# A two-layer encoder trunk on one core: latent projections moved to the start of each layer, on the input not yet divided by its RMS

## The chip, the cores and the metric

The kernel runs on one core of a Trainium2 chip. The metric is the device time of one execution in microseconds. The engines are TensorE (PE, with its weight loads as PEld), VectorE (DVE), ScalarE (ACT), GpSimd (POOL) and the DMA queues, of which SyncE (SP) issues all in the kernel before. Each engine works through its own instructions in order and waits on semaphores for the others.

## The reference, cut to what matters

```python
for l in range(DEPTH):                      # 2 layers, x is 256 x 1024, float32
    u = _rms_norm(x, pre_mix_norm_w[l])
    proj = u @ w_in[l]
    qkv_a, z_a, a_a, b_a, cq, ckv, k_rope, gate_logits = _split_cols(proj, PROJ_SIZES)
    qkv_a = jax.nn.silu(_causal_conv(qkv_a, conv_w[l]))
    # q_a, k_a l2-normalised per head; g_a from softplus(a_a), beta_a = sigmoid(b_a)
    o_a = _gated_delta_rule(q_a, k_a, v_a, g_a, beta_a)      # chunks of 64, 8 heads of 128
    o_a = _rms_norm(o_a, gdn_norm_w[l]) * jax.nn.silu(z_a)
    y_a = o_a @ w_branch_a[l]
    q_b = _rms_norm(cq, q_a_norm_w[l]) @ w_uq[l]             # cq: 384 wide; last 64 of a head rotated
    kv_b = _rms_norm(ckv, kv_a_norm_w[l]) @ w_ukv[l]         # ckv: 256 wide; k_rope: 64, rotated
    y_b = _chunk_causal_attention(q_b, k_b, v_b) @ w_branch_b[l]
    gates = jax.nn.sigmoid(gate_logits)
    h = gates[:, :, 0] * y_a + gates[:, :, 1] * y_b
    x = x + _rms_norm(h @ w_out[l], post_mix_norm_w[l])
    u = _rms_norm(x, pre_ffn_norm_w[l])
    x = x + _rms_norm(jnp.square(jax.nn.relu(u @ w_ff1[l])) @ w_ff2[l], post_ffn_norm_w[l])
```

`_rms_norm(x, w)` is x / sqrt(mean(x²) + 1e-6) times w.

## The kernel before, in words

All activations are held transposed, channels on the 128 partitions and the 256 tokens along the free dimension, so x is eight rows of 128 x 256. A product in float32 precision is made of three fast ones: each operand is split into a high part, rounded to the matmul's format, and a low part, the rest. High times high, high times low and low times high are summed in PSUM (lines 511 to 513). Weights arrive in pieces of 128 x 1024 (512 KB) in a ring of four buffers: ScalarE copies out the high part (`split_hi`, L908), VectorE subtracts it for the low part (`split_lo`, L1180), and SP then loads the next piece into the raw buffer. Of a split piece the buffers come free when TensorE has used it.

The work of a layer is a list of jobs (`JOBS`): v, q and k (4 jobs each, 2 pieces a job), `lat` (3 jobs: the key-value latent, then the query latent with the rotary key in the last half), `kn`, `vt` and `uq` (products of the normalised latents), z, gate, ya, yb, out, ff1 and ff2. A job of two pieces is 48 products of 256 columns into one of three PSUM banks in turn; then ScalarE or VectorE empties the bank. Between the jobs stand steps with small work. `schedule()` writes one order, by hand, and every engine walks this same list and does its part of each entry; `late` holds steps that are put in behind the next job (`job` calls `flush`). Splits are tied to the list as well: ahead of a job, both splitting engines first split up to four pieces past the job's last.

A layer opens with `sq` (ScalarE squares x), `sqsum` (VectorE adds), `norm` (TensorE sums over partitions with a matrix of ones, ScalarE takes the root by Ln and Exp, VectorE forms u and ScalarE and VectorE split it). v, q and k jobs follow, each with `conv` on VectorE and `silu` on ScalarE. The 16 gate inputs (a and b) come from 24 narrow products of their own weights behind v0 (`ab`, `logits`), and `gc` sums the log decays. Behind the k jobs come `lat` with `lnexp` (an explicit load of the table set for Ln and Exp), eight head norms `nrm` (POOL squares, TensorE sums, ScalarE Ln and Exp, VectorE multiplies), the latent norms `latn`, `ktrans`, four `decay` steps and `x1`, which prepares the inverse of the triangular matrices; `lvP` is its first product. The angles of the rotation are computed once, ahead of everything, by VectorE, and ScalarE takes the sines.

Of the kernel before, what the change touches and what calls it, by code (L numbers as in the profile page):

```python
# [23 lines left out]
P = 128  # L24
# [31 lines left out]
def jobs_of_a_layer():  # L56
# [3 lines left out]
    for kind, count, pieces in (("v", 4, 2), ("q", 4, 2), ("k", 4, 2), ("lat", 3, 2), ("kn", 4, 0.5), ("vt", 4, 0.5),  # L60
# [39 lines left out]
def schedule():  # L100

    o = [("start", 0), ("sq", 0), ("sq", 1), ("sqsum", 0), ("sq", 2), ("sq", 3), ("sqsum", 1), ("norm", 0)]
# [63 lines left out]
    def fillers():  # L166
        for i in range(1, 6):
# [21 lines left out]
    for _ in fill:  # L189
        pass  # L190
    o += [("sc", 0), ("sc", 1), ("onrm", 0), ("onrm", 1)]
    job("gate", 2)
    o += [("onrm", 2), ("onrm", 3)]
    for n in range(5):
        job("gate", 3 + n)
        if n:
            o.append(("pv", n - 1))
        o.append(("tr", n))
        if n + 2 < 6:
            o.append(("sc", n + 2))  # L200
# [3 lines left out]
    for i in range(4):  # L204
        job("ya", i)
        if i == 0:
            o += [("pv", 4), ("tr", 5)]
        if i == 1:
            o.append(("pv", 5))
# [25 lines left out]
ORDER = schedule()  # L235


def build(nc, x_in, pos_in, w_in, ab_in, prm_in, cst_in, out):
    with ExitStack() as ctx:
# [23 lines left out]
        prm = keep("prm", [P, NPRM])  # L263
# [4 lines left out]
        ab_all = keep("ab_all", [P, DEPTH, KD * 16])  # L268
        ab_hi = keep("ab_hi", [P, KD * 16], F32R)
        ab_lo = keep("ab_lo", [P, KD * 16], F32R)  # L270
# [4 lines left out]
        bias_cols = keep("bias_cols", [P, 2])  # L275
        eps_col, lnscale_col = bias_cols[:, 0:1], bias_cols[:, 1:2]
# [11 lines left out]
        ul = ph("ul", [P, KD, S], 8, F32R)  # L288
        qT = ph("qT", [P, H, S], 16)
# [13 lines left out]
        rl = ph("rl", [P, S], 83)  # L303
        latT = ph("latT", [P, 5, S], 84)
# [10 lines left out]
        abT = ph("abT", [16, S], 116)  # L315
# [31 lines left out]
        pos_i = ph("pos_i", [P, S], 0, I32)  # L347
        ang = ph("ang", [P, 4, S], 8)
# [26 lines left out]
        s_tab, s_x, s_in, s_out = S_("s_tab"), S_("s_x"), S_("s_in"), S_("s_out")  # L375
        s_trig, s_trig_a = S_("s_trig"), S_("s_trig_a")
# [11 lines left out]
        sq_sum_dve, sq_sum_pool = (signal("sq_sum_dve", 2), signal("sq_sum_pool", 2))  # L388
        x_by_pool, x_by_dve, y_add = (signal("x_by_pool", 4), signal("x_by_dve", 4), signal("y_add", 4))
        prm_ready, squared, sumsq, rnorm = (signal("prm_ready", 1), signal("squared", 8), signal("sumsq", 2), signal("rnorm", 4))  # L390
        pre_scaled, u_hi, u_lo, ab_split_hi = (signal("pre_scaled", 4), signal("u_hi", 4), signal("u_lo", 4), signal("ab_split_hi", 1))
        ab_t, ab_t_copied = (signal("ab_t", 1), signal("ab_t_copied", 1))
# [1346 lines left out]
```

## Time and profile before

| | us |
|---|---|
| median of 3 runs | 1131.35 |
| lowest, highest | 1130.5, 1137.35 |
| the profiled execution, its own time | 1130.21 |
| its span | 1128.1 |
| TensorE busy in the span | 1059.5 |
| VectorE, ScalarE, POOL busy | 745.2, 558.2, 149.6 |
| DMA, mean | 145 GB/s |

The span is the time between the first and the last recorded instruction. Matmuls overlap, so their recorded durations (some 280 ns) are longer than the distance from one to the next; where time is counted, the distance is used.

### The profile page before, as it was taken

What the parts mean: (1) busy time and instruction counts of PE and PEld (TensorE: products, weight loads), DVE (VectorE), ACT (ScalarE), POOL (GpSimd) and SP (SyncE); (2) the same over time, 40 slices, a digit from 0 to 9 for tenths busy, and PEclk for the clock granted to TensorE, in tenths of its full rate; (3) what the DMA queues carried; (4) which work ended last, traced back from release to release, by engine and by line L of the source; (5) the groups of instructions that cost most, each with busy time, mean ns of one, the idle gap of its engine ahead of it and who ended that gap; (6) DMA issues with size and microseconds to landing.
All of it is one profiled execution on the core that took longest, in us unless ns stands there. A gap on an engine that the chain in (4) does not pass through costs nothing.

```text
span 1128.1 us, 24201 instructions
## 1 busy us (share of the span) xinstructions
PE 1059.5 (94%) x10624; PEld 1021.3 (91%) x10624; DVE 745.2 (66%) x967; ACT 558.2 (49%) x766; POOL 149.6 (13%) x108
## 2 busy tenths in 40 slices
PE   3999988999999899999969999989999989999996
PEld 3999887999999799999869998879999989999996
DVE  7697764369767687744377878535696666876453
ACT  5556843635644554433256576445446345444341
POOL 0030310012000222200012114000310013221001
PEclk9999999999999999999969999999999998999998
DMA  5445323323466276666424452333235653666661
GB/s 190 153 158 176 124 95 96 115 74 113 138 207 190 85 214 183 189 187 184 127 94 149 151 168 95 132 96 114 61 127 171 185 168 99 211 187 194 187 184 42
DMA packets 45320, 163.98 MB, mean 145 GB/s; under 512 B 5152, under 2 KB 5536, under 8 KB 45088
## 3 DMA queue, kind: packets, MB, share of 16 engines
q1 hardware_dynamic: 45216, 162.44, 46.0%
q8 instruction: 84, 1.38, 0.5%
q14 instruction: 20, 0.16, 0.0%
HBM read 161.37 MB, written 1.05 MB: 144 GB/s over the span
## 4 chain that ended last, share of the span: by engine, by line
PE 76%; DVE 15%; ACT 5%; issue 3%; DMA 0%; POOLq 0%; POOL 0%; SPq 0%; DVEq 0%; ACTq 0%
PE dense L511 22%; PE dense L512 21%; PE dense L513 21%; DVE wlo L1180 4%; PE sides L607 1%; PE sides L738 1%; PE sides L730 1%; ACT rn L919 1%; DVE E L1402 1%; DVE yT L1463 1%; PE sides L648 1%; DVE E L1396 1%; DVE mx L1394 1%; ACT E L1114 1%; DVE E L1392 1%
## 5 line engine op out<-in xcount | busy, mean ns | idle before, releaser
L1180 DVE TENSOR_TENSOR wlo<-raw,whi 128x1024 fp32r<-128x1024 f32 (+1 forms) x304 | 402.1, 1338 | 187.3 <-ACT whi L908 186.8
L908 ACT ACTIVATE whi<-raw 128x1024 fp32r<-128x1024 f32 (+1 forms) x304 | 315.4, 1048 | 252.6 <-PE dense L513 250.9
L511 PE MATMUL dense<-uh,whi 128*128 128x256 f32 x864 | 254.7, 295 | 11.8 <-DVE ul L1205 7.1
L512 PE MATMUL dense<-ul,whi 128*128 128x256 f32 x864 | 245.9, 285 | 0.0
L513 PE MATMUL dense<-uh,wlo 128*128 128x256 f32 x864 | 245.9, 285 | 0.0
L511 PEld LDWEIGHTS dense<-uh,whi 128*128 128x128 f32 x864 | 166.7, 193 | 17.9 <-issue 13.2
L512 PEld LDWEIGHTS dense<-ul,whi 128*128 128x128 f32 x864 | 166.7, 193 | 2.1 <-issue 1.9
L513 PEld LDWEIGHTS dense<-uh,wlo 128*128 128x128 f32 x864 | 166.6, 193 | 0.0
L511 PE MATMUL dense<-fuh,whi 128*128 128x256 f32 x512 | 146.5, 286 | 10.5 <-DVE ful L1477 10.2
L512 PE MATMUL dense<-ful,whi 128*128 128x256 f32 x512 | 145.1, 283 | 0.0
L513 PE MATMUL dense<-fuh,wlo 128*128 128x256 f32 x512 | 145.1, 283 | 0.0
L513 PE MATMUL dense<-fh,wlo 128*128 128x256 f32 x512 | 143.5, 280 | 0.0
L512 PE MATMUL dense<-fl,whi 128*128 128x256 f32 x512 | 143.5, 280 | 0.0
L511 PE MATMUL dense<-fh,whi 128*128 128x256 f32 x512 | 143.5, 280 | 0.0
L511 PEld LDWEIGHTS dense<-fuh,whi 128*128 128x128 f32 x512 | 98.2, 192 | 12.3 <-issue 10.9
L512 PEld LDWEIGHTS dense<-ful,whi 128*128 128x128 f32 x512 | 98.4, 192 | 0.1
L513 PEld LDWEIGHTS dense<-fuh,wlo 128*128 128x128 f32 x512 | 98.1, 192 | 0.0
L511 PEld LDWEIGHTS dense<-fh,whi 128*128 128x128 f32 x512 | 96.4, 188 | 0.0
L513 PEld LDWEIGHTS dense<-fh,wlo 128*128 128x128 f32 x512 | 96.4, 188 | 0.0
L512 PEld LDWEIGHTS dense<-fl,whi 128*128 128x128 f32 x512 | 96.4, 188 | 0.0
L1610 POOL TENSOR_TENSOR fr<-fr 128x512 f32<-128x512 f32 x32 | 46.4, 1451 | 128.1 <-DVE fr L1449 128.1
L1577 POOL TENSOR_TENSOR sq<-sq,sq 128x512 f32<-128x512 f32 x8 | 10.4, 1297 | 323.4 <-ACT sq L1005 323.4
(272 smaller groups left out, 1861.5 us busy)
## 6 DMA issues: line engine op xcount, KB each, us to landing
raw<-weights SPq DMA_DIRECT2D x304, 512.0 KB, 4.1
xT<-x_t SPq DMA_DIRECT2D x1, 1024.0 KB, 5.3
out_t<-xT SPq DMA_DIRECT2D x4, 256.0 KB, 2.3
cst<-consts SPq DMA_DIRECT2D x1, 512.0 KB, 5.7
prm_all<-params SPq DMA_DIRECT2D x1, 150.0 KB, 5.3
pos_i<-pos SPq DMA_DIRECT2D x1, 128.0 KB, 2.1
ab_all<-w_ab SPq DMA_DIRECT2D x1, 128.0 KB, 6.0
cst<-consts SPq DMA_DIRECT2D x1, 2.0 KB, 1.9
```

The source lines that it names most:

```text
L511: mm(o_, h_[:, ws], ahi[:, k0 + k, :], start=is_first, stop=False, skip_group_check=True)
L512: mm(o_, h_[:, ws], alo[:, k0 + k, :], start=False, stop=False, skip_group_check=True)
L513: x_ = mm(o_, l_[:, ws], ahi[:, k0 + k, :], start=False, stop=is_last, skip_group_check=True)
L607: r = mm(side[0][:, 0:S], ones, q_[:, c, :], start=(c == 0), stop=(c == 5))
L648: r = mm(side[g % 3][:, e * P:(e + 1) * P], one_row, gcT[:, t * P:(t + 1) * P], start=True, stop=True)
L730: r = mm(side[e][rows, 16 * g:16 * (g + 1)], LT[rows, g, e, rows], evens(Xq[rows, e, g, :], SIZES[lv]), start=True, stop=True)
L738: r = mm(side[e][rows, 16 * g:16 * (g + 1)], XTq[rows, e, g, :], PBq[rows, e, g, 0:16], start=True, stop=True)
L908: return A(o_, i_, ACT.Copy)
L919: A(out_, in_, ACT.Ln, scale=scale, bias=eps_col).then_inc(rises, 1)
L1114: A(E[n % 2][:], E[n % 2][:], ACT.Exp, scale=float((DK + ROPE) ** -0.5)).then_inc(sm_exp, 1)
L1180: TT(wlo[s][:, 0:w], raw[s][:, 0:w], f32(whi[s][:, 0:w]), ALU.subtract).then_inc(lo_ready, 1)
L1610: G(fr[i % 4][:], fr[i % 4][:], fr[i % 4][:], ALU.mult).then_inc(f_sq, 1)
```

## The change

The `lat` jobs become the first of each layer. They run on x times its gain, split into `xh` and `xl`, without the division by the RMS r. Since the latent norms would divide it out again, only their epsilon has to be scaled: the argument of the root becomes mean(lat²) + 1e-6 r², with `xm` = 1e-6 r² taken as an Exp. The rotary key and the gate inputs are multiplied by 1/r when the bank is emptied. The 16 gate inputs move into the last lat block (its 48 spare columns are zeros); their own weights, products, copy and DMA go. The norm of x stands behind lat 0. Residual addition and split of the next layer's x are interleaved. The rotary key's step `kr` and POOL's `qd` become steps of their own, further back. The angles are computed by POOL, with the sines behind `silu` 0; x is loaded in four parts on SP, parameters, positions and constants on ScalarE's queue. The last ff2 job also splits two pieces of the next layer. Some attention steps stand one job further back.

```diff
-    for kind, count, pieces in (("v", 4, 2), ("q", 4, 2), ("k", 4, 2), ("lat", 3, 2), ("kn", 4, 0.5), ("vt", 4, 0.5),
+    for kind, count, pieces in (("lat", 3, 2), ("v", 4, 2), ("q", 4, 2), ("k", 4, 2), ("kn", 4, 0.5), ("vt", 4, 0.5),
...
-    o = [("start", 0), ("sq", 0), ("sq", 1), ("sqsum", 0), ("sq", 2), ("sq", 3), ("sqsum", 1), ("norm", 0)]
+    o = [("xsplit", 0), ("xsplit", 1)]
...
+    job("lat", 0)
+    o += [("sq", 0), ("sq", 1), ("sqsum", 0), ("sq", 2), ("sq", 3), ("sqsum", 1), ("norm", 0)]
+    job("lat", 1)
+    o.append(("latn", 0))
+    job("lat", 2)
+    o += [("logits", 0), ("latn", 1)]
     for i in range(4):
         job("v", i)
+        o.append(("conv", i))
         if i == 0:
-            o.append(("ab", 0))
-        o.append(("conv", i))
-        if i == 1:
-            o += [("logits", 0), ("silu", 0)]
-        if i:
+            o += [("gc", 0), ("silu", 0), ("trig", 0)]
+        else:
             late.append(("silu", i))
-        if i == 3:
-            o.append(("gc", 0))
...
         late.append(("silu", 8 + i))
         if i == 0:
             o += [("vtrans", 3), ("dt", 3)]
-    job("lat", 0)
     o += [("lnexp", 0), ("nrm", 0), ("nrm", 1)]
-    job("lat", 1)
-    o += [("nrm", 2), ("latn", 0), ("nrm", 3)]
-    job("lat", 2)
+    job("kn", 0)
+    o += [("nrm", 2), ("nrm", 3)]
+    job("kn", 1)
+    job("kn", 2)
     o += [("nrm", 4), ("nrm", 5)]
-    job("kn", 0)
-    o += [("nrm", 6), ("nrm", 7)]
-    job("kn", 1)
-    o.append(("ktrans", 0))
-    job("kn", 2)
-    o += [("ktrans", 1), ("latn", 1)]
     job("kn", 3)
-    o += [("decay", 0), ("decay", 1)]
     job("vt", 0)
-    o.append(("decay", 2))
+    o += [("nrm", 6), ("nrm", 7), ("qd", 0), ("kr", 0), ("ktrans", 0)]
     job("vt", 1)
+    o += [("ktrans", 1), ("decay", 0), ("decay", 1), ("decay", 2)]
+    job("vt", 2)
     o += [("decay", 3), ("zero", 0), ("x1", 0)]
-    job("vt", 2)
     job("vt", 3)
     job("uq", 0)
+    job("uq", 1)
...
-                for c in (0, 1, 4, 5):
+                for c in (0, 1, 4, 5) if w else (0, 1):
...
             def logits(l, _):
 
-                pe.wait_ge(ab_t_copied, due(l, ab_t_copied, 1))
+                pe.wait_ge(dve_evac, l * NDVE_EVAC + evacs_through(FIRST["lat"] + 2)[1])
...
+            def xsplit(l, part):
+
+                for e in (range(2), range(2, KD))[part]:
+                    if e % 2 == 0:
+                        x_there(l, 0, e // 2)
+                    if l == 0 and e == 0:
+                        act.wait_ge(s_prm, 16)
+                    A(xh[:, e, :], xT[:, e, :], ACT.Identity,
+                      scale=prm_all[:, l, PRE_MIX + e:PRE_MIX + e + 1]).then_inc(x_hi, 1)
...
+            def trig(l, _):
+                if l == 0:
+                    act.wait_ge(s_trig, 24)
+                    A(cosT[:], ang[:, 0, :], ACT.Sin).then_inc(s_trig_a, 1)
+                    A(sinT[:], ang[:, 1, :], ACT.Sin).then_inc(s_trig_a, 1)
...
+            def x_low(l, e):
+                dve.wait_ge(x_hi, due(l, x_hi, e + 1))
+                STT(xl[:, e, :], xT[:, e, :], col(l, PRE_MIX + e), f32(xh[:, e, :]), ALU.mult, ALU.subtract).then_inc(x_lo, 1)
...
+                if n:
+                    dve.wait_ge(sq_sum_dve, due(l, sq_sum_dve, 2))
+                    TT(usq[:, 0:2, :], usq[:, 0:2, :], usq[:, 4:6, :], ALU.add).then_inc(sq_sum_dve, 1)
...
+                dve.wait_ge(lat_mm, due(l, lat_mm, n + 1))
+                dve.wait_ge(x_mean, due(l, x_mean, 1))
+                if n:
+                    dve.wait_ge(lat_norm, due(l, lat_norm, 1))
+                STT(rl[:], side[4][:, 0:S], 1.0 / (QL if n else KVL), xm[:], ALU.mult, ALU.add).then_inc(lat_arg, 1)
...
                 times_norm(0)
+                add(0)
                 times_norm(1)
-                add(0)
+                low(0)
                 times_norm(2)
-                low(0)
-                times_norm(3)
                 add(2)
                 low(1)
+                times_norm(3)
                 low(2)
                 low(3)
```

## Rows read from the trace of the kernel before

**Rows 1.** The page: span, busy time of an engine, and one group of instructions

```profile
span 1128.1 us, 24201 instructions
PE 1059.5 (94%) x10624; PEld 1021.3 (91%) x10624; DVE 745.2 (66%) x967; ACT 558.2 (49%) x766; POOL 149.6 (13%) x108
...
L908 ACT ACTIVATE whi<-raw 128x1024 fp32r<-128x1024 f32 (+1 forms) x304 | 315.4, 1048 | 252.6 <-PE dense L513 250.9
```

**Rows 2.** TensorE's waits over the whole span: total us, times, longest

```profile
PE sides L607 <- DVE usq L1192: 21.2, 2, 13.6
...
PE dense L511 <- DVE wlo L1180: 4.4, 4, 1.2
```

**Rows 3.** The chain that ended last, 0 to 120 us: start, us, what

```profile
13.56 3.76 PE sides L607 x8
...
20.84 0.55 PE dense L511
21.39 0.21 PE dense L512
```

**Rows 4.** The same chain, 540 to 720 us, where layer 1 opens

```profile
561.93 0.48 ACT rn L919
...
576.83 0.55 PE dense L511
```

**Rows 5.** Busy time by stretch: PE, PEld, DVE, ACT, POOL, clock, DMA share, GB/s

```profile
80.00:100.00 20.00, 20.00 (x170) 19.71 (x170) 15.31 (x26) 12.22 (x21) 0.00 (x0) 1.00 0.45 144
104.10:156.80 52.70, 48.97 (x336) 42.58 (x335) 38.94 (x65) 38.20 (x62) 15.18 (x12) 1.00 0.35 111
```

**Rows 6.** ScalarE in order of time: start, us, line, operation

```profile
11.54 2.19 ACT L928 ACTIVATE usq<-xT 128x512 f32<-128x512 f32 x4
...
110.42 0.62 ACT L1010 ACTIVATE kT<-kT 128x512 f32<-128x512 f32 x1
111.06 1.28 ACT L1018 ACT_TABLE_LOAD   x1
112.35 0.23 ACT L1021 ACTIVATE sm<-sm 128x32 f32<-128x32 f32 x1
...
112.61 0.67 ACT L919 ACTIVATE rn<-sides,bias_cols 128x512 f32<-128x512 f32 x1
...
115.27 1.99 ACT L908 ACTIVATE whi<-raw 128x1024 fp32r<-128x1024 f32 x2
```

**Rows 7.** VectorE in order of time, in four stretches

```profile
10.73 0.24 DVE L1186 COPY prm<-prm_all 128x150 f32<-128x150 f32 x1
...
18.42 1.67 DVE L1209 SCALAR_TENSOR_TENSOR utmp<-xT,prm,rn 128x256 f32<-128x256 f32 x4 [1.35 <-ACT rn L921]
...
24.19 0.28 DVE L1215 TENSOR_TENSOR ab_lo<-ab_all,ab_hi 128x128 fp32r<-128x128 f32 x1
...
31.70 0.41 DVE L1219 COPY abT<-sides 16x256 f32<-16x256 f32 x1 [3.20 <-PE sides L619]
...
56.41 3.84 DVE L1180 TENSOR_TENSOR wlo<-raw,whi 128x1024 fp32r<-128x1024 f32 x2
...
567.58 1.29 DVE L1186 COPY prm<-prm_all 128x150 f32<-128x150 f32 x1
```

**Rows 8.** Groups of ScalarE's instructions: busy us, mean ns, idle before

```profile
L1010 ACT ACT_TABLE_LOAD x2 | 2.6, 1283 | 0.0
```

**Rows 9.** The chain that ended last, 120 to 300 us

```profile
145.55 0.22 PE sides L708 x2
...
156.81 1.25 PE sides L730 x84
```

**Rows 10.** DMA issues of the page: KB each, median us to landing

```profile
raw<-weights SPq DMA_DIRECT2D x304, 512.0 KB, 4.1
...
out_t<-xT SPq DMA_DIRECT2D x4, 256.0 KB, 2.3
```

More of the change, by code:

```diff
@@ L166, in fillers @@
     def fillers():
-        for i in range(1, 6):
+        for i in range(2, 6):
             job("uq", i)
@@ L190, in schedule @@
         pass
+    job("gate", 2)
     o += [("sc", 0), ("sc", 1), ("onrm", 0), ("onrm", 1)]
-    job("gate", 2)
+    job("gate", 3)
     o += [("onrm", 2), ("onrm", 3)]
-    for n in range(5):
-        job("gate", 3 + n)
+    for n in range(4):
+        job("gate", 4 + n)
         if n:
             o.append(("pv", n - 1))
-        o.append(("tr", n))
-        if n + 2 < 6:
-            o.append(("sc", n + 2))
+        o += [("tr", n), ("sc", n + 2)]
         if n < 2:
@@ L235, with build @@
 ORDER = schedule()
-def build(nc, x_in, pos_in, w_in, ab_in, prm_in, cst_in, out):
+assert [n for what, n in ORDER if what == "job"] == list(range(NJOB))
+def build(nc, x_in, pos_in, w_in, prm_in, cst_in, out):
     with ExitStack() as ctx:
@@ L891, in ysum @@
                 r.then_inc(y_mm, 1)
-            do = dict(norm=norm, ab=ab, logits=logits, dt=dt, job=job, gc=gc, vtrans=vtrans, nrm=nrm, latn=latn, ktrans=ktrans, decay=decay,
+            do = dict(norm=norm, logits=logits, dt=dt, job=job, gc=gc, vtrans=vtrans, nrm=nrm, latn=latn, kr=kr_, ktrans=ktrans, decay=decay,
                       lvP=lvP, lvV=lvV, pairP=pairP, pairV=pairV, lastP=lastP, lastV=lastV, half=half, t_v0=t_v0, t_st=t_st, t_ks=t_ks, t_v1=t_v1, t_o=t_o, onrm=onrm,
                       sc=sc, tr=tr, pv=pv, ysum=ysum, qrope=qrope)
-            pe.wait_ge(s_in, 3 * 16)
             for l in range(DEPTH):
@@ L1147, in fsplit @@
                 copy(fh[:, 2 * i:2 * i + 2, :], fr[i % 4][:]).then_inc(f_hi, 1)
-            do = dict(sq=sq_, squares=squares, norm=norm, fsplit_x=fsplit_x, logits=logits, job=job, silu=silu, vtrans=vtrans, lnexp=lnexp, nrm=nrm, latn=latn,
+            do = dict(xsplit=xsplit, trig=trig, sq=sq_, squares=squares, norm=norm, fsplit_x=fsplit_x, logits=logits, job=job, silu=silu, vtrans=vtrans, lnexp=lnexp, nrm=nrm, latn=latn,
                       decay=decay, x1=x1, pairP=pairP, pairV=pairV, lastP=lastP, lastV=lastV, t_st=t_st, t_o=t_o, onrm=onrm, osplit=osplit, sc=sc, tr=tr, pv=pv, sig=sig,
                       hsplit=hsplit, post=post, fsplit=fsplit)
-            act.wait_ge(s_trig, 12)
-            A(cosT[:], ang[:, 0, :], ACT.Sin).then_inc(s_trig_a, 1)
-            act.wait_ge(s_trig, 20)
-            A(sinT[:], ang[:, 1, :], ACT.Sin).then_inc(s_trig_a, 1)
-            act.wait_ge(s_x, 16)
-            nc.scalar.preload_act_table_set("natural_log_exp_and_others")
+            nc.scalar.preload_act_table_set("natural_log_exp_and_others")
+            act.dma_start(prm_all[:], prm_in).then_inc(s_prm, 16)
+            act.dma_start(pos_i[:], pos_in).then_inc(s_tab, 16)
+            act.dma_start(cst[:, C_FREQ:NCST], cst_in[:, C_FREQ:NCST]).then_inc(s_tab, 16)
+            act.wait_ge(s_x[1], 16)
+            act.dma_start(cst[:, 0:C_FREQ], cst_in[:, 0:C_FREQ]).then_inc(s_in, 16)
+            act.wait_ge(s_bias, 3)
             for l in range(DEPTH):
-                for (what, n), pieces in zip(ORDER, splits_at):
+                for (what, n), pieces in steps_with_splits(l):
                     for p_ in pieces:
-                        split_hi(l, p_)
+                        split_hi(p_)
                     if what in do:
@@ L1494, in fsplit @@
                    f32(fh[:, 2 * i:2 * i + 2, :]), ALU.subtract).then_inc(f_lo, 1)
-            do = dict(start=start, sqsum=sqsum, norm=norm, ab=ab, logits=logits, gc=gc, dt=dt, conv=conv, nrm=nrm, latn=latn, qrope=qrope, ktrans=ktrans,
+            do = dict(xsplit=xsplit, sqsum=sqsum, norm=norm, logits=logits, gc=gc, dt=dt, conv=conv, nrm=nrm, latn=latn, kr=kr_, qrope=qrope, ktrans=ktrans,
                       decay=decay, x1=x1, lvP=lvP, lvV=lvV, t_v0=t_v0, t_v1=t_v1, t_ks=t_ks, onrm=onrm, osplit=osplit, sc=sc, pv=pv, job=job,
@@ L1529, in _ @@
-            dve.wait_ge(s_trig_a, 2)
-            step(TS(sinT[:], sinT[:], cst[:, C_FREQ + 1:C_FREQ + 2], None, ALU.mult))
-            dve.wait_ge(s_x, 16)
-            dve.wait_ge(s_in, 3 * 16)
+            V.memset(eps_col, EPS).then_inc(s_bias, 1)
+            V.memset(lnscale_col, math.log(DK ** -0.5)).then_inc(s_bias, 1)
+            V.memset(lneps_col, math.log(EPS)).then_inc(s_bias, 1)
+            dve.wait_ge(s_prm, 16)
             for l in range(DEPTH):
-                for (what, n), pieces in zip(ORDER, splits_at):
+                for (what, n), pieces in steps_with_splits(l):
```

331 lines of the change are left out of this document (171 added, 160 removed).

## The prediction, on record before the changed kernel ran

> **What bounds the kernel now.** I read the page first: TensorE is busy 94% of the span and ScalarE 49% [rows 1], so the end moves with TensorE's work and its idle time, and with nothing else. The list of waits then says where TensorE idles for another engine: 21.2 us in two waits at the sum of squares that opens a layer, 4.4 us in four for split weights [rows 2]. The chain of waits dates the openings. In layer 0 the norm's products run 13.56 to 17.32 and the first dense product starts at 20.84 [rows 3]; in layer 1 the last sum of layer 0 ends at 561.93, where ScalarE takes over, and the first dense product starts at 576.83 [rows 4]. Products there come 0.21 us apart (1.2 GHz, after TensorE had been idle); in steady state 170 in 20 us, 0.118 us apart (2.4 GHz) [rows 3, 5], so a dense job of 48 costs 5.65 us. Last I looked at the stretch out of which the latent jobs are taken, from the end of the k jobs to the first product of the triangular inverse, 104.1 to 156.8. TensorE is busy 49.0 of its 52.7 us, ScalarE 38.2 [rows 5]: the latent jobs are what fills TensorE while ScalarE works through eight norms.
>
> **The openings.** Before, v0 runs 20.84 to 28.6 and the 24 gate-input products end at about 31.4 (the copy behind them starts at 31.70 [rows 7]). After, x comes in 256 KB parts, first in the queue; a store of that size takes 2.3 us and a weight piece 4.1 [rows 10]. The piece, issued fifth at about 2.6, lands near 7; its split (1.05 on ScalarE [rows 1], some 1.2 on VectorE) lets TensorE start near 9.4 (13.5 if it lands as late as 11). lat0 then takes 7.8 us, as v0 did, to 17.2. But the norm is behind lat0 in every queue: ScalarE waits for lat0, squares the bank (0.6), then x four times (2.19 [rows 6]), VectorE adds three times (1.4 of it after the last square): 21.4. Two of four norm products are left, 1.9 us: 23.3.
>
> From there a chain decides, not TensorE. VectorE normalises x (1.35 for the root, 5.8 for eight products and four low halves, 18.42 to 24.19 [rows 7]), ScalarE splits pieces 5 and 6 only behind it (2.1), VectorE follows with 2.5 and lat1's evacuation 0.8; first latent norm 3.3 over both engines; pieces 7 and 8, 2.8; lat2's evacuation 0.8; logits and second sum 1.9: about 19.7 us, while TensorE has 14.1 of work. v0 would start at 43.0. Before, the same work (norm, three jobs, latent sums 2.2) stands at 31.4 + 11.3 + 2.2 = 44.9.
>
> Into this falls the angle chain, 24 dependent steps on POOL. A POOL instruction holds VectorE up: a copy of 150 columns that takes 0.24 takes 1.29 beside POOL's add, and two splits take 3.84 beside the DT chain [rows 7] instead of twice 1.2. No row has POOL's scalar step. Four of its 512-column operations cost VectorE some 3 us, so 24 of half that width cost at most 9 and, where VectorE has slack, nothing; I take 2. Layer 0 gains 1.9 - 2 = 0 (bounds -7 and +6).
>
> Layer 1: rn at 562.9, first add at 564.2, xh and xl of the first row at 565.2, TensorE starts at 565.3 instead of 576.8 (pieces 0 and 1 are split during the last ff2 job). lat0, mostly at 1.2 GHz and paced by the adds, ends at 573.2. The same late squares put the norm's products at 578.6 and the chain puts v0 at 600.2; before, 587.6 + 11.3 + 2.2 = 601.1. Gain 1 (0 to +5). **So 11.5 us of earlier start per layer come back as two new waits**: some 5 us at the norm, 3.4 at the logits.
>
> The trade shows in VectorE's queue too: the add for xh waits behind lat0's evacuation, and the logits step now waits for lat2's evacuation, with v0 queued behind it. In the v jobs the logits chain no longer delays splits (2.2 us a layer, half of the 4.4 [rows 2]); layer 0 gets the two sines there instead, with a table load before and one after, 3.4 us of ScalarE. I take -2.0 for both layers.
>
> **The middle.** This is the largest term. Taken out of the stretch: three jobs, 16.95, and 10 latent products, 2.2; drawn in: uq1, 18 products, 2.1. Net 17.0 us of TensorE per layer that stand elsewhere; the stretch must shrink by 17.0 to come out even.
>
> silu(11) is appended behind the last k job and issued at the next job. That was lat0, ahead of lnexp(0): Silu at 110.42, the table load at 111.06 [rows 6]. Now it is kn0, and lnexp(0), nrm 0 and nrm 1 stand before it. So ScalarE loads the table for Ln and Exp, does two norms, loads Silu's (at line 1010 a load stands that nobody wrote [rows 8]), and meets Ln again in nrm 2 with Silu's set active. What set an unwritten load for Ln brings no row shows. Low bound: the shared one, two loads more. High bound: one that lacks Exp; then every Ln and Exp of nrm 2 to 7 loads, 12 + 1 = 13. I take the high bound: the source asks for Sigmoid by function, but before every stage that alternates Ln and Exp it asks for the set by name (lines 1018, 1135, 1157), which would be needless if asking for Ln brought both. At 1.283 us each [rows 8], 16.7 us per layer on the engine that paces the norms.
>
> ScalarE's queue from the end of k3: evacuation and silu 10, 2.0; written load and two small Exps 1.6; nrm 0 and 1, 2.65 (112.61 to 115.27 [rows 6]); splits 33 to 35, 2.45; five evacuations 2.4; silu 11 and two qd exponentials 1.5; nrm 2 to 7, 6 x 1.33 = 8.0; 13 loads 16.7: 37.3. TensorE's and VectorE's parts are shorter and each nrm waits for the last Ln. Then in series: last kT product 0.7, ktrans 0.7, decay 0 to 3 of 16 products at 0.11 [rows 9] 4 x 1.78, vt2 1.4, decay 3 on VectorE 1.65, x1 4.9 (the last decay ends near 151.9, the inverse starts at 156.81 [rows 9]): 16.5. That is 53.8; TensorE has then been idle often, and what of it runs at 1.2 GHz adds 0 to 3: 55.3. The stretch grows by 2.6 where it should shrink by 17.0: **loss 19.6 per layer, 39.2** (low bound, two loads: the same walk gives 39.7 for the stretch, a loss of 4.0 per layer).
>
> **Small ones.** The residual step before ff1 reaches its first low half one 0.6 us multiplication earlier: -1.2 for two layers. The last POOL add (1.64) starts one such instruction later: +0.6. kr's work is about equal, the gate inputs' dropped DMA and the prm copy lie beside other work; the attention steps moved behind gate and ya jobs keep 5.65 us of product each as cover: 0; without it a step waits for its softmax, some 3 us.
>
> **Sum**, against the profiled execution's 1130.2: 0 - 1.0 - 2.0 + 39.2 - 1.2 + 0.6 = +35.6: 1165.8. The median of the runs is 1131.35, 1.1 above it: **1167**.
>
> **The skill beside it.** The Trainium skill (ScalarE: Activation LUTs, What ACT_TABLE_LOAD costs) adds a drain of 1.38 us to each switch. Here 111.06 + 1.283 = 112.34 and the next activation starts at 112.35 [rows 6], so the trace disagrees. The same page's rule to group calls by table set speaks against this order. The Trainium skill (GPSIMD Engine Reference, Key points) has GpSimd share its memory interfaces with VectorE; the 1.29 beside 0.24 agrees.
>
> **Rivals.**
> Shared set: the load before nrm 2's Ln brings both. Then 8 stands for 39.2: 1130.2 - 1.0 - 2.0 + 8 - 1.2 + 0.6 = 1134.6, with the median 1136. For it: every load in the trace stays good for a whole stage. Against: the sets named by hand. 0.08.
> Faster: the opening gains survive. Place: between TensorE's early start and v0. If the chain of 19.7 shrinks to TensorE's 14.1 and the wait at the norm stays under 2, each layer keeps 5.6 + 3 more; with shared loads that is 1136 - 17 = 1119. It decides from a chain near 14 us; VectorE's own part of it, 5.8 + 2.5 + 0.8 + 1.7 + 2.5 + 0.8 = 14.1, speaks against. 0.04.
> Slow clock: the idle middle keeps TensorE at 1.2 GHz, so that its 9.2 us of products in series take double (7.7 more than I allowed, per layer), and POOL costs the opening its 7: 1167 + 15 + 7 = 1189. 0.05.
> Drain: each of 26 new loads costs 1.38 more, 1203. 0.01.
> Forecast 0.82. The change does what it says in all of them.
>
> **Range.** Own range: the middle 34 (no slow clock, and a load or two per layer hidden in a wait) to 47, the openings 10 better to 7 worse, the rest 2 either way: 1150 to 1184. It leaves out the rivals and little more. A run of this kernel can tell 1% (11 us) from nothing; slower by over 1%: forecast, slow clock, drain and a part of shared set, 0.89; within: 0.07; faster 0.04.
>
> **What would show it.** Table loads at the norm's Ln and Exp lines, 12 per layer; from the end of k3 to the first inverse product 53 to 58 us with TensorE busy about 31; first dense product near 9.4 and 565, a wait of about 5 behind lat0 and 3 before the logits. It is wrong if loads number two a layer there, or if the stretch ends near 40.

## The result, and the profile after

The changed kernel takes 1188.63 us (median of 4 runs, 1185.69 to 1192.16), the kernel before 1133.05 beside it; the ratio is 1.0488 [1.0442, 1.0534]. The direction was right, the size was not: 1167 was predicted, in a range of 1150 to 1184, so the loss is 55.6 us between these medians and 58.8 between the profiled executions (1130.21 to 1188.98), where the sum had 35.6.

The first rows of the page after, against [rows 1]: TensorE is busy 12 us longer, and idle 46.8 us more (115.4 against 68.6).

```profile
span 1186.8 us, 24158 instructions
PE 1071.4 (90%) x10568; PEld 1027.8 (87%) x10568; DVE 754.3 (64%) x967; ACT 598.2 (50%) x807; POOL 167.4 (14%) x133
```

The list of TensorE's waits after (what waited, for whom: us in total, times, longest) answers [rows 2]. The two waits of 21.2 us are gone. The first row is four waits: 10.7 at the kernel's start, 3.3 in the first latent job of layer 1, and 5.0 ahead of ya0 in either layer. In place of the old two stand 12 waits for Ln in the norms of q and k, one per layer ahead of the key transposes, and in the opening one for the sum of squares and one for the rotary key.

```profile
PE dense L515 <- DVE wlo L1206: 24.0, 4, 10.7
PE sides L669 <- ACT rn L919: 20.6, 12, 3.4
PE sides L693 <- DVE kT L1303: 12.8, 2, 6.9
PE sides L624 <- DVE krx L1468: 9.7, 2, 5.0
PE dense L515 <- DVE ful L1514: 9.6, 2, 4.8
PE sides L617 <- DVE usq L1228: 8.7, 2, 4.4
```

ScalarE's table loads after, by line (count, total us, mean ns), answer [rows 8]: twelve per layer at the norms' Ln (L919) and Exp (L921), and a second per layer at silu (L1029).

```profile
L919 ACT ACT_TABLE_LOAD x12 | 15.4, 1283 | 0.2
L921 ACT ACT_TABLE_LOAD x12 | 15.4, 1283 | 0.2
L1029 ACT ACT_TABLE_LOAD x4 | 5.1, 1283 | 0.1
L1043 ACT ACT_TABLE_LOAD x4 | 5.1, 1283 | 0.1
```

ScalarE's timeline in the middle of layer 0 (start, duration) shows how it comes about, where [rows 6] had one load for the whole stage. Silu's set is fetched for the last k pair; from then on every Ln fetches one set and every Exp another.

```profile
130.49 0.72 ACT L921 ACTIVATE rn<-rn,bias_cols 128x512 f32<-128x512 f32 x1
...
132.66 1.28 ACT L1029 ACT_TABLE_LOAD   x1
133.95 0.63 ACT L1029 ACTIVATE kT<-kT 128x512 f32<-128x512 f32 x1
134.60 1.28 ACT L919 ACT_TABLE_LOAD   x1
135.89 0.69 ACT L919 ACTIVATE rn<-sides,bias_cols 128x512 f32<-128x512 f32 x1
136.60 1.28 ACT L921 ACT_TABLE_LOAD   x1
137.89 0.72 ACT L921 ACTIVATE rn<-rn,bias_cols 128x512 f32<-128x512 f32 x1
```

The same stretch as a window, from the end of k3 to the first product of the inverse, in both layers (length; busy us of TensorE, its weight loads, VectorE, ScalarE, POOL; granted clock; DMA share and rate), answers [rows 5]. It lasts 57.1 us (55.3 predicted, against 52.6 before), ScalarE works 46 of them, TensorE's granted clock is 0.79 and 0.82.

```profile
125.00:182.10 57.10, 39.73 (x199) 30.19 (x197) 28.01 (x51) 45.94 (x62) 13.40 (x12) 0.79 0.18 56
705.50:762.50 57.00, 38.64 (x198) 29.43 (x197) 28.00 (x51) 45.96 (x62) 13.40 (x12) 0.82 0.17 55
```

TensorE's waits in the two openings, as its timeline after has them (start, duration, and in brackets the idle time before and who ended it): at the norm, at the logits, and in layer 1 inside lat0, for the second weight piece. v0 starts at 47.51 and 629.13.

```profile
23.17 1.19 PE L617 MATMUL sides<-usq,cst 128*128 128x256 f32 x2 [4.38 <-DVE usq L1228]
44.19 1.03 PE L624 MATMUL sides<-cst,krx 16*128 16x16 f32 x4 [4.97 <-DVE krx L1468]
...
596.48 0.58 PE L515 MATMUL dense<-xh,whi 128*128 128x256 f32 x1 [3.30 <-DVE wlo L1206]
606.26 1.19 PE L617 MATMUL sides<-usq,cst 128*128 128x256 f32 x2 [4.30 <-DVE usq L1228]
```

Last, a place where the prediction had put nothing: ahead of ya0. After gate 7 ScalarE does the sixth softmax's Exp, loads Sigmoid's table, does four sigmoids and loads the other table back; only then come the two splits that ya0 needs. VectorE's low half and TensorE's wait follow.

```profile
323.69 0.63 ACT L1139 ACTIVATE E<-E 128x512 f32<-128x512 f32 x1 [4.28 <-DVE E L1432]
324.34 1.28 ACT L1154 ACT_TABLE_LOAD   x1
325.63 3.90 ACT L1159 ACTIVATE gates<-gates 128x1024 f32<-128x1024 f32 x4
329.55 1.28 ACT L1160 ACT_TABLE_LOAD   x1
330.84 2.00 ACT L908 ACTIVATE whi<-raw 128x1024 fp32r<-128x1024 f32 x2
...
331.93 2.36 DVE L1206 TENSOR_TENSOR wlo<-raw,whi 128x1024 fp32r<-128x1024 f32 x2 [5.97 <-ACT whi L908]
...
333.21 0.58 PE L515 MATMUL dense<-oh,whi 128*128 128x256 f32 x1 [4.98 <-DVE wlo L1206]
```

### The profile page after: what moved, and what is told of

It is laid out like the page before. It is cut to its first block, busy times and chain, and to the rows that moved or that the text cites. A ratio compares the mean times of both kernels' runs of the same rounds, so it can differ in the third digit from the quotient of the medians.

```text
span 1186.8 us, 24158 instructions
## 1 busy us (share of the span) xinstructions
PE 1071.4 (90%) x10568; PEld 1027.8 (87%) x10568; DVE 754.3 (64%) x967; ACT 598.2 (50%) x807; POOL 167.4 (14%) x133
## 3 DMA queue, kind: packets, MB, share of 16 engines
q8 instruction: 83, 1.36, 0.5%
## 4 chain that ended last, share of the span: by engine, by line
PE 73%; DVE 13%; ACT 9%; issue 4%; DMA 0%; POOL 0%; SPq 0%; POOLq 0%; ACTq 0%; DVEq 0%
PE dense L515 21%; PE dense L517 20%; PE dense L516 20%; DVE wlo L1206 4%; ACT L919 1%; ACT whi L908 1%; ACT rn L919 1%; PE sides L739 1%; ACT rn L921 1%; PE sides L731 1%; PE sides L709 1%; PE sides L710 1%; PE sides L646 1%; DVE E L1432 1%; DVE mx L1430 1%
## 5 line engine op out<-in xcount | busy, mean ns | idle before, releaser
L515 PE MATMUL dense<-uh,whi 128*128 128x256 f32 x768 | 223.7, 291 | 0.1
L516 PE MATMUL dense<-ul,whi 128*128 128x256 f32 x768 | 216.3, 282 | 2.7 <-issue 2.7
L517 PE MATMUL dense<-uh,wlo 128*128 128x256 f32 x768 | 215.8, 281 | 2.4 <-issue 2.4
L516 PEld LDWEIGHTS dense<-ul,whi 128*128 128x128 f32 x768 | 145.9, 190 | 4.2 <-issue 3.8
L515 PEld LDWEIGHTS dense<-uh,whi 128*128 128x128 f32 x768 | 146.1, 190 | 3.7 <-issue 1.4
L517 PEld LDWEIGHTS dense<-uh,wlo 128*128 128x128 f32 x768 | 146.2, 190 | 2.6 <-issue 2.6
L1587 POOL TENSOR_TENSOR sq<-sq,sq 128x512 f32<-128x512 f32 x8 | 10.4, 1296 | 320.3 <-ACT sq L1024 320.3
```

The lines of the kernel that those rows point to most:

```text
L515: mm(o_, h_[:, ws], ahi[:, k0 + k, :], start=is_first, stop=False, skip_group_check=True)
L516: mm(o_, h_[:, ws], alo[:, k0 + k, :], start=False, stop=False, skip_group_check=True)
L517: x_ = mm(o_, l_[:, ws], ahi[:, k0 + k, :], start=False, stop=is_last, skip_group_check=True)
```

## Where the 58.7 us of span went

The stages are cut at the same products in both traces; work that changed its stage is taken out as in the prediction (17.0 us out of the middle, 19.1 into the opening, 2.1, uq1, out of the inverse).

| stage, both layers | predicted | measured |
|---|---|---|
| opening, up to v0 | -1.0 | +8.4 (2.6 and 5.8) |
| v, q, k jobs | -2.0 | -3.2 |
| middle | +39.2 | +43.1 (21.6 and 21.5) |
| inverse, attention, up to ff1 | -1.2 | +16.5 (6.0 and 10.5) |
| ff1, ff2, tail | +0.6 | -6.1 |
| sum | +35.6 | +58.7 |

Not all of this repeats. The changed kernel was profiled a second time (further down); its opening, jobs and middle take the same times within 1 us, but the fourth row of the table would be +13.3 there (3.0 in layer 0, 10.4 in layer 1): 3 us of layer 0's 6.0 belong to the one execution.

## Experiments: the middle

Theory: the loads pace the middle. Rival: without the latent jobs the middle is starved anyway. First the last silu ahead of the named set:

```diff
+    flush()
     o += [("lnexp", 0), ("nrm", 0), ("nrm", 1)]
     job("kn", 0)
```

> The changed kernel with the last k pair's silu issued ahead of the named table set instead of behind the second norm. Theory (table loads pace the middle): the 12 loads per layer at the norm's Ln and Exp and the two around the silu fall to 1 or 2, ScalarE's queue loses some 15.4 to 16.7 us per layer, so the stretch from the end of the k jobs to the first product of the inverse falls from 57.3 to 40 to 42 us in both layers and the run from 1188.6 to 1154 to 1160. Rival (the middle is starved, because the latent jobs that filled it are gone, whatever ScalarE does): the stretch stays above 50 and the run above 1175.

Measured: 1158.49 us, 1.0258 [1.0228, 1.0288] times the kernel before; the stretch takes 41.74 and 41.75 us, and no load stands at the norms. The theory holds, and the rival falls as the cause of the 57 us; what it says of the missing jobs may still hold for the 6 us per layer that are left (41.75 against 52.6 - 17.0). 30 of the 58 us are this one line.

Then the order kept, and the set asked for by name again:

```diff
     job("kn", 0)
-    o += [("nrm", 2), ("nrm", 3)]
+    o += [("lnset", 0), ("nrm", 2), ("nrm", 3)]      # preload_act_table_set("natural_log_exp_and_others")
```

> The changed kernel with only the table set asked for by name once more behind that silu, the order kept. Theory: 2 loads per layer more than with the silu ahead of the set (one for the silu, one back), each 1.283 us on ScalarE's queue, but no wait of ScalarE for the last convolution in front of the first norms, so 0 to 3 us per layer from the run with the silu ahead: 1154 to 1164, with 0 loads at the lines of the norm's Ln and Exp. Rival (starved middle): above 1175.

Measured: 1156.83 us, 1.0243 [1.0198, 1.0287]. In its windows ScalarE is busy 31.3 of 41.0 us instead of 46 of 57, and TensorE's clock stays at or near 1.00:

```profile
125.70:166.70 41.00, 32.87 (x199) 25.18 (x198) 28.61 (x51) 31.32 (x51) 13.12 (x12) 1.00 0.24 78
689.30:730.30 41.00, 34.12 (x203) 26.54 (x204) 28.45 (x51) 31.48 (x51) 13.56 (x12) 0.96 0.24 77
```

So 11 loads fewer per layer, 14.1 us of ScalarE, shorten the stretch by 16.1; the other 2.0 go with TensorE's granted clock (0.79 and 0.82 before this edit) and were not taken apart. What is left of the middle's loss is 41.0 - (52.6 - 17.0) = 5.4 us per layer.

The same silu moved in the kernel before, where the latent jobs still stand in the middle:

```diff
-    job("lat", 0)
+    o.append(("job", FIRST["lat"]))                  # no flush: silu 11 stays queued
     o += [("lnexp", 0), ("nrm", 0), ("nrm", 1)]
     job("lat", 1)
```

> The kernel before with only its last silu moved behind the second norm, as the change has it. Theory: 12 loads per layer at the norm's Ln and Exp here too, 16.7 us more on ScalarE, which was busy 38.2 of the 52.7 us of the stretch; the latent jobs cover part of it, and the stretch grows to 60 to 67: the run 1147 to 1160. Rival (with its latent jobs in place the stretch hides the loads): the stretch below 56, the run below 1140.

Measured: 1173.42 us, 1.0393 [1.0374, 1.0412]; the stretch takes 74.8 us in both layers, 22.3 more. Both expectations were too low, for two reasons that its rows show: there are 16 loads per layer at the norms, since the two latent norms stand in the middle too, and one more at silu (17 x 1.283 = 21.8), and 49 us of TensorE's work cover none of them.

```profile
L919 ACT ACT_TABLE_LOAD x16 | 20.5, 1283 | 0.3
L921 ACT ACT_TABLE_LOAD x16 | 20.5, 1283 | 0.3
L1010 ACT ACT_TABLE_LOAD x4 | 5.1, 1283 | 0.1
...
104.00:178.90 74.90, 55.39 (x340) 46.27 (x338) 37.14 (x65) 60.59 (x79) 14.24 (x12) 0.89 0.24 78
```

## Experiments: the opening

The steps put in the order in which their inputs come:

```diff
+    o += [("sq", 0), ("sq", 1), ("sqsum", 0), ("sq", 2), ("sq", 3), ("sqsum", 1)]
     job("lat", 0)
-    o += [("sq", 0), ("sq", 1), ("sqsum", 0), ("sq", 2), ("sq", 3), ("sqsum", 1), ("norm", 0)]
     job("lat", 1)
-    o.append(("latn", 0))
+    o += [("norm", 0), ("latn", 0)]
     job("lat", 2)
-    o += [("logits", 0), ("latn", 1)]
...                                                  # ("logits", 0), ("latn", 1) behind v0, ("gc", 0), ("silu", 0), ("trig", 0) behind v1
-            return 1 if (what, n) == ("xsplit", 1) else 0
+            return l * NPIECE + 1 + (l > 0) if (what, n) == ("xsplit", 1) else 0
```

> The kernel with the silu ahead of the table set (1158.5), and besides the opening reordered: the squares of x and their sums ahead of the first latent job, the norm's products behind the second, the logits and the second latent norm behind v0, and in layer 1 the second weight piece split along with the copies of x. Theory (TensorE's waits at the norm, 4.4 us, and at the logits, 4.9 us, in each layer, and for the second piece's split in layer 1, 3.4 us, come from the place of these steps in the queues): from the first latent product to v0 36.6 us falls to 25 to 29 in layer 0 and 40.5 to 26 to 31 in layer 1, the run to 1134 to 1142. Rival (the chain of norm, split and evacuation on VectorE and ScalarE sets v0 whatever the order): v0 comes at most 6 us earlier in the two layers together and the run stays above 1150.

Measured: 1144.46 us, 1.0140 [1.0114, 1.0166], 14.0 less than with the silu repair alone (1158.49). v0 starts 22.9 and 25.7 us behind the first latent product (36.6 and 40.5 with the old order), earlier than the theory asked. But v0 itself now takes 11.3 us in layer 0, since the splits of its weights stand behind the norm's copies: 3.7 us of it is a wait for `wlo` (2.8 in layer 1). At the end of k3 5.8 and 8.7 us are left. The run missed the theory's 1134 to 1142 and is under the rival's 1150. Both theories are half right: the order made the waits, and behind them the queues of VectorE and ScalarE set the pace.

The second weight piece of layer 1 alone, on top of the silu repair (only the last edit above):

> The kernel with the silu ahead of the table set (1158.5), and besides only the second weight piece of layer 1 split along with the copies of x. Theory: the wait for split weights in the first latent job of layer 1, 3.4 us, goes; lat0 of layer 1 takes 10 instead of 13.4 us, but the norm's products still wait for the sums, so of these 3.4 at most 1 reaches v0: 1157 to 1158.5, and the gap at the norm grows. Rival (the chain behind lat0 moves with it): v0 of layer 1 3 us earlier, 1155.

Measured: 1159.33 us, 1.0236 [1.0197, 1.0275], and v0 of layer 1 0.5 us earlier: nothing to be had. Its timelines of ScalarE, VectorE and TensorE say why. The high half is made at 576.15, the low half not before 583.43, since it stands behind all eight low halves of x in VectorE's queue; TensorE's wait shrinks from 2.90 to 2.48 only.

```profile
576.15 1.04 ACT L909 ACTIVATE whi<-raw 128x1024 fp32r<-128x1024 f32 x1
...
582.63 0.88 DVE L1214 SCALAR_TENSOR_TENSOR xl<-xT,prm_all,xh 128x256 fp32r<-128x256 f32 x2 [0.29 <-ACT xh L939]
583.43 4.63 DVE L1207 TENSOR_TENSOR wlo<-raw,whi 128x1024 fp32r<-128x1024 f32 x4
...
584.70 0.38 PE L516 MATMUL dense<-xh,whi 128*128 128x256 f32 x1 [2.48 <-DVE wlo L1207]
```

The changed kernel with 4 of POOL's 24 angle steps; it leaves out the reduction of the angles, so its outputs are not the reference's:

```diff
-            for dst, shift, add in ((0, 0.25, 0.5 * math.pi), (1, 0.0, 0.0)):   # 11 steps each
+            for dst in (0, 1):
+                step(GS(A_(dst), A_(2), PI_BELOW, -PI_BELOW, ALU.min, ALU.max))
```

> The changed kernel with the range reduction of the angles left out: GpSimd makes 4 steps instead of 24 (the angles are then clamped, not reduced, which changes the outputs). Theory (GpSimd's steps hold VectorE up through the opening of layer 0, and so the norm's chain): VectorE's norm of x in layer 0 takes as long as in layer 1, v0 starts 2 to 4 us earlier than 47.5, layer 1 keeps its times, the run is 2 to 4 us shorter. Rival (VectorE has slack there, the waits at the norm and the logits are set by the order alone): v0 at 47 to 47.5 and no difference in the run.

Measured: 1180.41 us (1175.51 to 1191.15), too wide for 2 us; the trace decides. v0 of layer 0 starts at 45.56 instead of 47.51, k3 ends 1.5 us earlier; in layer 1 v0 starts 40.5 us behind the first latent product, as in the second profile of the changed kernel (40.4). Four products of VectorE's norm take 2.39 us beside POOL's steps and 1.67 without them (first row after, second here):

```profile
26.61 2.39 DVE L1242 SCALAR_TENSOR_TENSOR utmp<-xT,prm_all,rn 128x256 f32<-128x256 f32 x4 [3.59 <-ACT rn L959]
```

```profile
26.13 1.67 DVE L1242 SCALAR_TENSOR_TENSOR utmp<-xT,prm_all,rn 128x256 f32<-128x256 f32 x4 [3.59 <-ACT rn L959]
```

## Experiments: attention and inverse

The order of attention as before, in the changed kernel:

```diff
-    job("gate", 2)
     o += [("sc", 0), ("sc", 1), ("onrm", 0), ("onrm", 1)]
+    job("gate", 2)
...                                                  # and so on to ya1: sc 5 behind gate 6, not behind gate 7
```

> The changed kernel with the order of gate jobs, scores, softmax transposes and values of the kernel before put back, the rest left. Theory (the sixth softmax now ends behind gate 7 without a job to cover it, so that the sigmoids, and the weight split queued behind them on ScalarE, start late): the wait for split weights at ya 0 falls from 5.3 us to 1.3 in both layers, the run gets 8 us shorter, 1181. Rival (the lost 4 us come from the extra gate job before the scores or from the clock): the run stays within 2 us of 1188.6.

Measured: 1180.74 us, 1.0439 [1.0395, 1.0484], 7.9 less than the changed kernel; from the first product of the inverse to yb0 164.8 and 169.2 us instead of 168.9 and 174.5. The wait at ya0 is 1.25 in both layers, where the changed kernel has 4.98, so the two waits are 7.5 of the 7.9 us. (The other 1.9 us by which these stretches differ are less than the 3 us by which two executions of the changed kernel differ there.)

```profile
331.59 0.39 PE L516 MATMUL dense<-oh,whi 128*128 128x256 f32 x1 [1.25 <-DVE wlo L1207]
912.71 0.38 PE L516 MATMUL dense<-oh,whi 128*128 128x256 f32 x1 [1.25 <-DVE wlo L1207]
```

All three repairs (silu, opening, attention) in one kernel:

> The three repairs together: silu ahead of the table set, opening reordered, attention order of the kernel before. If their prices add (31, some 20, 8 us off 1188.6): 1126 to 1135, level with the kernel before at 1130.4 or up to 4 us under it. If the gains of an earlier v0 are lost in the middle, which ScalarE paces: 1140 or more.

Measured: 1133.82 us (12 runs, 1130.66 to 1139.29), 1.0039 [1.0024, 1.0054]. The prices add: 30.1 + 14.0 + 7.9 = 52.0 off 1188.63 would give 1136.6. In its profiled execution the end of k3 stands 3.3 (layer 0) and 5.5 us (layer 1) earlier than before, counted for the moved 19.1, so the early start does pay; the middle takes back 6.0 per layer (41.6 against 52.6 - 17.0).

The same with uq1 back among the fillers:

```diff
     job("uq", 0)
-    job("uq", 1)
...
-        for i in range(2, 6):
+        for i in range(1, 6):
```

> The three repairs together, and the second uq job back among the fillers of the inverse. Theory (the stretch of the inverse lost its time because each step got a longer filler and the middle gained a job that nothing waits for): the stretch from the last k job to the first product of the inverse is 2 to 2.5 us shorter, the stretch from there to the scores 2 to 2.5 longer, the run the same within 2 us. Rival (the extra 4 us of layer 1 in the inverse, gaps of some 2 us inside runs of small products that the profile puts down to issue, come from the shifted fillers): these gaps fall to the 3.7 us of the kernel before and the run gets 3 to 5 us shorter.

Measured: 1137.66 us, 1.0067 [1.0038, 1.0097]. Both were wrong. The stretch of the middle is not shorter (41.75 and 41.51 with or without uq1), because the inverse's first product waits there for VectorE's last transpose (3.21 us, and 1.09 with uq1 ahead of it): uq1 was free cover. From the first product of the inverse to the scores it takes 87.9 us in both layers, against 82.1 and 88.7 without it among the fillers: 5.0 more in sum, where uq1's own work is 4.2.

Two edits to the middle on top of the repairs: the reload by name with the last decay and the copies for the inverse ahead of vt2, and then also the kn banks emptied by VectorE:

```diff
-    job("vt", 2)
     o += [("decay", 3), ("zero", 0), ("x1", 0)]
+    job("vt", 2)
```

> The three repairs, with the table set asked for by name again behind the silu instead of the silu put first, and the last decay and the copies for the inverse ahead of the third vt job. Theory: 0.7 us per layer from the reload (41.0 against 41.75 in the stretch), 1 to 1.4 per layer because a vt job no longer stands in series: the stretch 39.5 to 40 in both layers, the run 1129 to 1131 where all three repairs gave 1133.8. Rival (the inverse then waits for the same copies, since they have less cover): the stretch 41 or more, the run 1132 to 1135.

Measured: 1137.08 us (12 runs, 1129.87 to 1141.44), 1.0050 [1.0029, 1.0071]; stretch 41.26 in both layers. The stretch is the rival's (41 or more), its mechanism is not: the inverse waits for the copies no longer (the 1.09 us are gone), but uq1 now waits 0.87 us for a bank that ScalarE empties behind them. Of the 1.7 to 2.1 us per layer that were expected 0.3 to 0.5 came.

```diff
-EVAC_BY_ACT = {"v", "q", "k", "uq", "kn", "vt", "z"}
+EVAC_BY_ACT = {"v", "q", "k", "uq", "vt", "z"}
...                                                  # VectorE's copy of the kn bank, and the scores' wait for it
```

> The three repairs, with the table set asked for by name again behind the silu instead of the silu put first, the last decay and the copies for the inverse ahead of the third vt job, and the four kn evacuations on VectorE instead of ScalarE. Theory (the middle is paced by ScalarE's queue until the last norm, and then by steps in series): to the kernel with the first two of these (the next run) it adds 2 us per layer less on ScalarE between the norms: 1125 to 1129, under the kernel before (1130.2). Rival (VectorE, which sits in the same chain between two norms, takes the evacuations in its place): no gain over the next run.

Measured: 1131.45 us (12 runs, 1126.88 to 1140.97), 1.0017 [0.9992, 1.0042]; stretch 40.3 and 40.1, so 1.1 us per layer where 2 were expected, and the run is not under the kernel before, where 1125 to 1129 were expected. This is the best version of the change that was run, level with the kernel before. None beat it.

## Experiments: what repeats

Layer 0's feed-forward stage ran 7 us faster after than before, with nothing in the change to explain it. The changed kernel once more:

> The changed kernel once more, to see what repeats. If the faster products of layer 0's feed-forward stage (179 in 20 us against 172, both at a granted clock of 1.00) and the gaps inside runs of small products in the inverse belong to this program: the same stages show them again, first ff1 product to last ff2 product 179.2 us in layer 0 and 186.0 in layer 1. If they belong to an execution: they stand elsewhere or are gone (some 186 in both layers).

Measured: one execution, 1185.14 us. Windows of 20 us in the two feed-forward stages, first the changed kernel's profile, then this one (the number in brackets behind TensorE's busy time counts its products, 179 or 172):

```profile
500.00:520.00 20.00, 20.00 (x179) 20.00 (x178) 10.95 (x11) 8.14 (x10) 0.00 (x0) 1.00 0.68 211
1090.00:1110.00 20.00, 20.00 (x172) 20.00 (x172) 10.24 (x10) 7.91 (x8) 0.00 (x0) 1.00 0.69 211
```

```profile
500.00:520.00 20.00, 20.00 (x172) 20.00 (x172) 10.24 (x11) 8.22 (x9) 0.00 (x0) 1.00 0.61 198
1090.00:1110.00 20.00, 20.00 (x179) 20.00 (x178) 10.02 (x11) 8.68 (x9) 0.00 (x0) 1.00 0.66 213
```

The fast stage has moved to layer 1. It belongs to an execution, not to the program: over the profiles of this study the stage takes 178.5 to 179.6 us or 184.6 to 186.2, and never between; the granted clock is 1.00 in all four windows above. So the 6 us of the table's last row say nothing of the change.

The gaps without a releaser in the inverse (the profile ends them with "issue") are in part another matter. In layer 1 they sum to 4.1 us before (5.3 with its silu moved) and to 5.3 to 8.6 in the kernels with the change; the changed kernel has 7.6 and, the second time, 7.7. In layer 0 they sum to 4.0 before and 3.4 to 5.6 after, and there one program gave 5.3 and then 3.7. Where they stand is fixed: 127 or 128 products apart or a multiple of it, each product with its weight load, so some 256 instructions. Counted from TensorE's first product in the program, gaps of layer 0 stand at 1353, 1480 and 1862 both in the kernel before, whose inverse begins at product 1002, and in the second profile of the changed one, where it begins at 992; in layer 1 one stands at 6536 with all three repairs and also with uq1 back, where the inverse begins 18 products earlier. Two kernels shift the stream behind the first product of layer 1's inverse:

```diff
+                if l == 1 and lv == 0:
+                    for b, g, e, rows in list(quads())[:64]:      # or [:32]; the same product as below
+                        mm(side[e][rows, 16 * g:16 * (g + 1)], LT[rows, g, e, rows], evens(Xq[rows, e, g, :], SIZES[lv]), start=True, stop=True)
                 for b, g, e, rows in quads():
```

> The kernel with all three repairs, and in layer 1 alone the first 64 small products of the first step of the inverse issued twice (the same values into the same place, some 0.4 us of work). What it tests: TensorE's gaps without a releaser in the inverse stand 127 or 128 products apart, in layer 1 of the changed kernels 132 and 260 products behind the step's first one, in layer 0 at 234, 361 and 488, in the kernel before at 349 and 476. Theory (the gaps stand where the instruction stream is fetched in blocks, and their sum depends on where the blocks fall among the small products): the gaps move to 132 and 260 counted with the 64 repeated ones, so 64 products earlier in the work, and their sum in the first 95 us of layer 1 changes from 7.2 us to somewhere between 3.4 and 8. Rival (the gaps belong to these steps and the data they wait for): they stay at the same products, 196 and 324 counted with the repeated ones, with the sum at 7.2 and the run 0.4 us longer.

> The same with 32 of the small products issued twice. Theory (blocks): the block ends then fall at 100, 228 and 356 products of the work, nearly where layer 0 and the kernel before have them (106, 234, 361; 94, 221, 349), and the sum of the gaps in layer 1 falls from 7.2 us to 3.4 to 5.6, as in layer 0; layer 1 from the first product of the inverse to the scores takes 85 to 87 us instead of 88.7. Rival (layer 1 loses these us for another reason): the sum stays at 6 to 8.

A call of `mm` makes two products in the trace: the first kernel has 128 products more than the one with all three repairs (10696 against 10568), not the 64 of its expectation, and the second 64 (10632). So 128, a whole distance between gaps, brings every later gap back to the same work, and only the second kernel shifts them against it. TensorE's first gaps in layer 1 with all three repairs, then with 128, then with 64 repeated products:

```profile
719.87 0.28 PE L519 MATMUL dense<-latl,whi 128*128 128x256 f32 x1 [1.28 <-issue]
726.16 0.41 PE L742 MATMUL sides<-PBq,XTq 32*32 32x16 f32 x14 [3.47 <-issue]
```

```profile
724.36 1.89 PE L738 MATMUL sides<-Xq,LT 32*32 32x16 f32 x123 [2.43 <-issue]
729.60 0.37 PE L519 MATMUL dense<-latl,whi 128*128 128x256 f32 x1 [2.21 <-issue]
```

```profile
726.98 1.04 PE L738 MATMUL sides<-Xq,LT 32*32 32x16 f32 x59 [2.32 <-issue]
740.59 1.16 PE L746 MATMUL sides<-PBq,XTq 32*32 32x16 f32 x116 [1.49 <-issue]
```

Counted from the step's first product (repeated ones included) the gaps stand at 132 and 260 in the first, at 133 and 260 with 128 repeated, at 133 and 514 with 64. They stayed at their place in the stream and so moved back in the work: they belong to the stream. Their size does not follow from their place: at 260 it is 0.9 to 4.0 us in the kernels with the change, and in two of them there is no gap. The sums are 7.2 without, 8.6 with 128 and 6.1 with 64. The last is more than the 3.4 to 5.6 expected for it, though its stretch up to the scores, 86.9 us, lay in the expected 85 to 87; the 8.6 with no later gap shifted says that a sum can move by over 1 us without a shift of the later gaps. In time: 1143.81 us with 128, 1.0116 [1.0092, 1.0140]; 1135.38 with 64, 1.0024 [1.0001, 1.0047]. Why layer 1 of the changed kernels loses more in these gaps stays open.

The Trainium skill (Runtime: NRT & Kernel Launch, Instruction fetch mechanics) has instructions fetched in blocks of 256. The spacing agrees, and so does the page of the profile after, whose instruction queue moved 1.36 MB in 83 packets, 16.4 KB each. It calls the crossing mostly hidden; here, where 128 small products last 1.2 us, it shows with up to 4.0 us.

## Why the prediction was wrong, by its own steps

**The middle: right in kind, 1.8 us short per layer.** The high bound held: an unwritten load for Ln brings a set without Exp, 12 loads at Ln and Exp, 13 in all counting silu's. Its rival of a shared set is excluded by the rows. ScalarE's queue from the end of k3 to the last Exp took 37.8 us (37.3 predicted). The walk without these loads gave 39.7; with them gone 41.0 was measured, so 1.3 of the 1.8 were in the walk.

**The opening: the wait at the norm and the one at the logits came as predicted in place, and larger.** The chain from the norm's products to v0 took 23.1 us in layer 0 (24.4 to 47.5) and 21.7 in layer 1, not 19.7; POOL's part was 2.0 of the first, as allowed (2). Here the prediction added wrongly: the terms that it lists come to 21.4, not 19.7, and with 21.4, and 2.0 for POOL in layer 0, the chain is met within 0.3 us in both layers. In layer 1 the step that failed besides was "pieces 0 and 1 are split during the last ff2 job": `ahead = 2` reaches one piece past the job's last, not two, so only piece 0 was (the description of the change makes the same slip), and lat0 ended at 601.96, 14.2 us behind its first product, not 8 (its term "paced by the adds"). This is the larger part of that layer's 5.8. The experiment on this piece shows that its split alone was no cause: with the high half made in time the low halves of x, in the same queue of VectorE, hold it up nearly as long (2.48 us for 2.90).

**The v jobs: -3.2 for -2.0.** The sines needed no table of their own, which the prediction had put at 3.4 us of ScalarE:

```profile
58.47 0.63 ACT L1029 ACTIVATE vT<-vT 128x512 f32<-128x512 f32 x1 [1.30 <-DVE vT L1292]
59.00 0.40 ACT L1034 ACTIVATE cosT<-ang 128x256 f32<-128x256 f32 x1
59.31 0.40 ACT L1035 ACTIVATE sinT<-ang 128x256 f32<-128x256 f32 x1
```

**Attention: this step failed outright.** "The attention steps moved behind gate and ya jobs keep 5.65 us of product each as cover: 0; without it a step waits for its softmax, some 3 us." That holds for each softmax but the sixth. It now begins behind gate 7, the last job ahead of the sigmoids, and what waits is not its own transpose but everything behind its Exp in ScalarE's queue. Priced by putting the order back: 7.9 us. The prediction followed the moved steps on TensorE and not on the queue that they share with the sigmoids and the weight splits.

**The inverse: no step at all; the prediction put it at nothing.** After attention's 8, 8.5 of the 16.5 us remain. 4.8 are gaps of TensorE without a releaser (1.3 and 3.5 us more than before), of which the cause in this kernel is open; 3.7 were not assigned. In the second profile of the same kernel 5.3 remain, 3.3 of them such gaps, all in layer 1: what repeats is layer 1's 3.5 us.

**The feed-forward stage** gave 6 us back in this execution, and in the second one too, there in layer 1; in the kernel before neither layer had the fast stage. That hid part of the miss.

The rival "slow clock" named nearly the measured time, 1189, but not its way: of the products in series behind the last norm of layer 0 only the sums of kT and the first 20 of the decay steps came at 1.2 GHz (those 20 stand 0.21 us apart instead of 0.11, some 2 us more), and POOL cost 2, not 7. That its number came near is chance. The forecast's mechanism was the largest cause; the two misses that carried the time out of the range were the opening (9.4 us more than its -1.0) and the attention order (7.9 for 0).

## What to carry to other kernels

Where a list of steps is written out by hand, a step that is "issued at the next job" moves when the next job does: one silu issued behind the table set and two norms cost 30 of the 58 us, in a change that never mentions it. An activation of another table set ahead of alternating Ln and Exp cost one load per call here (12 and 16 per layer), until the set was asked for by name again (none), and TensorE's work did not cover it. Follow a moved step through every queue that it stands in and look at what is behind it there, above all at the last one of a series, which has lost the cover that the others keep.

## What the runs showed of the hardware that was not expected

Sin ran directly behind Silu without a table load (59.00 behind 58.47). The same program ran whole stages at 0.112 us or at 0.116 us per product (20 us by 179 or by 172) with the granted clock at 1.00 both times. And 128 more small products, 1.2 us of work, came with a kernel 10 us longer (1143.81 against 1133.82; 1.0116 [1.0092, 1.0140] against 1.0039 [1.0024, 1.0054] of the kernel before). The gaps do not explain it: they are 1.3 us longer in sum. In the two profiled executions, 6.4 us apart, 3.4 us of the difference stand in layer 0, ahead of the edit. No run here shows the cause. So a difference under 1% between two such programs can't be put down to the edit from the times alone, even when it is clear of the runs' scatter; the trace has to show it at the place of the edit.
